# Where the split weights and the split input lie in the on-chip memory of a two-block transformer kernel

## The reference

```python
# block 1
h = rmsnorm(x, norm_mix);  p = h @ w_in                    # 2048 x 4352
x = x + concat([pool_mixer(p), hyena_mixer(p), gated_mixer(p)]) @ w_out
h = rmsnorm(x, norm_ffn);  up = dwconv3(h @ ffn_w_up)      # 2048 x 11264
x = x + (silu(gate) * val) @ ffn_w_down                    # 5632 x 2048
x = rmsnorm(x, norm_final)
# block 2
x = x + rmsnorm(fox_attention(rmsnorm(x, g0), fox_w_in, fox_w_out), g1)
x = x + rmsnorm(square(relu(rmsnorm(x, g2) @ mlp_w1)) @ mlp_w2, g3)   # 2048 x 8192, 8192 x 2048
```

## Time and profile before

| | us |
|---|---|
| three timed runs: median (lowest, highest) | 2157.93 (2157.85, 2158.72) |
| the profiled execution: its own time | 2158.86 |
| the profiled execution: span of the trace | 2157.0 |
| TensorE busy (matmuls) | 2148.6 |
| TensorE's loads of stationary operands, busy | 1864.5 |
| VectorE busy | 1303.6 |
| ScalarE busy | 1009.5 |
| GpSimd busy | 64.5 |

### The profile page before, as it was taken

The page is one execution under the profiler, slowest core; times in us unless marked ns, Lnnn a source line. Parts: engine busy times, 40 slices in busy tenths (PEclk is TensorE's granted clock), DMA queues, the critical chain, the costliest instruction groups (busy, mean ns, idle before and its releaser), DMA issues.

```text
span 2157.0 us, 27987 instructions
## 1 busy us (share of the span) xinstructions
PE 2148.6 (100%) x11694; PEld 1864.5 (86%) x11694; DVE 1303.6 (60%) x1611; ACT 1009.5 (47%) x1186; POOL 64.5 (3%) x85
## 2 busy tenths in 40 slices
PE   9999999999999999999999999999999999999999
PEld 7888888888888888888898889888888888888887
DVE  6868557776777775444655665466555555444445
ACT  6444446545545554444655444455434334444443
POOL 3030000000000000000001010000000000000000
PEclk9999999999999999999999999999999999999999
DMA  9655656566555655555566555546666665555552
GB/s 338 213 172 176 215 183 204 180 196 195 192 184 186 195 181 198 194 194 195 165 205 205 158 176 184 199 144 215 184 189 195 185 188 194 195 195 195 193 190 104
DMA packets 268925, 412.41 MB, mean 191 GB/s; under 512 B 6981, under 2 KB 247045, under 8 KB 250112
## 3 DMA queue, kind: packets, MB, share of 16 engines
q1 hardware_dynamic: 265648, 398.08, 56.6%
q0 software_dynamic: 2432, 11.75, 1.5%
q10 hardware_dynamic: 720, 0.79, 0.1%
HBM read 408.49 MB, written 2.11 MB: 190 GB/s over the span
## 4 chain that ended last, share of the span: by engine, by line
PE 97%; DMA 1%; DVE 1%; ACT 1%; SPq 0%; issue 0%; ACTq 0%; DVEq 0%
PE bank L1546 35%; PE bank L1559 18%; PE bank L1607 11%; PE bank L1608 11%; PE bank L1612 11%; PE bank L1549 2%; PE bank L1561 2%; PE bank L1550 2%; DMA M<-in_xt 1%; PE bank L1441 1%; PE bank L1398 0%; DMA X<-in_x 0%; DVE M L1304 0%; PE bank L1524 0%; PE bank L1491 0%; PE bank L1477 0%
## 5 line engine op out<-in xcount | busy, mean ns | idle before, releaser
L800 DVE TENSOR_TENSOR wlo<-raw,whi 128x2048 fp32r<-128x2048 f32 (+1 forms) x372 | 852.5, 2293 | 760.5 <-ACT whi L480 760.4
L480 ACT ACTIVATE whi<-raw 128x2048 fp32r<-128x2048 f32 (+1 forms) x371 | 710.3, 1916 | 781.5 <-PE bank L1612 421.3
L1546 PE MATMUL bank<-hh,whi 128*128 128x512 f32 x3360 | 807.2, 392 | 0.6 <-ACT whi L480 0.6
L1546 PEld LDWEIGHTS bank<-hh,whi 128*128 128x128 f32 x3360 | 618.3, 188 | 123.5 <-ACT whi L480 1.0
L1559 PEld LDWEIGHTS bank<-hh,wlo 128*128 128x128 f32 x3360 | 430.7, 191 | 16.3
L1559 PE MATMUL bank<-hh,wlo 128*128 128x256 f32 x3360 | 436.0, 283 | 0.0
L1607 PE MATMUL bank<-whi,hh 128*128 128x512 f32 x1072 | 417.6, 390 | 0.0
L1608 PE MATMUL bank<-whi,hh 128*128 128x512 f32 x1072 | 417.1, 389 | 0.0
L1612 PE MATMUL bank<-wlo,hh 128*128 128x512 f32 x1072 | 264.8, 389 | 0.0
L1607 PEld LDWEIGHTS bank<-whi,hh 128*128 128x128 f32 x1072 | 201.2, 188 | 41.9 <-DVE M L868 0.2
L1612 PEld LDWEIGHTS bank<-wlo,hh 128*128 128x128 f32 x1072 | 201.2, 188 | 41.8
(11 more groups left out here) (247 smaller groups left out, 941.8 us busy)
## 6 DMA issues: line engine op xcount, KB each, us to landing
raw<-in_mlp_w SPq DMA_DIRECT2D x128, 1024.0 KB, 5.5
raw<-in_ffn_w_up SPq DMA_DIRECT2D x88, 1024.0 KB, 5.1
raw<-in_ffn_w_down SPq DMA_DIRECT2D x44, 1024.0 KB, 4.8
raw<-in_fox_w_in SPq DMA_DIRECT2D x32, 1024.0 KB, 5.4
raw<-in_w_in SPq DMA_DIRECT2D x31, 1024.0 KB, 5.5
raw<-in_fox_w_in SPq DMA_DIRECT2D x16, 1032.0 KB, 5.4
raw<-in_w_out SPq DMA_DIRECT2D x16, 1024.0 KB, 4.8
raw<-in_fox_w_out SPq DMA_DIRECT2D x16, 1024.0 KB, 4.8
```

The lines of the kernel that those rows point to most:

```text
L480: e.activation(whi[i % RING][:, 0:n], raw[i % RAW][:, 0:n], ACT.Copy).then_inc(s_hi, 1)
L800: e.tensor_tensor(wlo[i % RING][:, 0:n], raw[i % RAW][:, 0:n], whi[i % RING][:, 0:n].bitcast(F), ALU.subtract).then_inc(s_lo, 1)
L1546: e.matmul(bank[b][:, :], wh[:, k, s], hh[:, kk, :], start=kk == 0, stop=False)
```

## The change

The order of the allocations changes, and where the unused bytes stand. All of it is in the list of tensors at the start of `two_block_program`; no instruction is added, removed or moved on any of the five engines, only the addresses in them change (and, by 7, the line numbers behind the list).

```diff
-        st = sb("st", [P, 80])
-        raw = [sb("raw0", [P, UN])]
-        whi, wlo = [], []
-        for i in range(RING):
-            whi.append(sb(f"whi{i}", [P, UN], R))
-            raw.append(sb(f"raw{i + 1}", [P, UN]))
-            gap(2 * i, 96)
-            wlo.append(sb(f"wlo{i}", [P, UN], R))
-            if i == 0:
-                edge = sb("edge", [P, 64])
-            gap(2 * i + 1, 48 if i == 0 else 112)
-        hh = sb("hh", [P, KD, 2 * T], R)
+        tiles = {}
+        for name, before, shape, dt in (
+                ("rb", 0, [P, T], F),
+                ("raw0", 0, [P, UN], F),
+                ("wlo2", 24, [P, UN], R),
+                ("whi2", 32, [P, UN], R),
+                ("whi0", 0, [P, UN], R),
+                ("raw2", 0, [P, UN], F),
+                ("raw3", 0, [P, UN], F),
+                ("cols", 0, [P, NCOL], F),
+                ("wlo0", 72, [P, UN], R),
+                ("wlo1", 0, [P, UN], R),
+                ("edge", 0, [P, 64], F),
+                ("raw1", 0, [P, UN], F),
+                ("hh", 8, [P, KD, 2 * T], R),
+                ("whi1", 0, [P, UN], R),
+                ("st", 0, [P, 80], F),
+                ("end", 24, [P, 8], F)):
+            if before:
+                sb(f"before_{name}", [P, before])
+            tiles[name] = sb(name, shape, dt)
+        st, edge, rb, cols, hh = (tiles[n] for n in ("st", "edge", "rb", "cols", "hh"))
+        raw = [tiles[f"raw{i}"] for i in range(RAW)]
+        whi, wlo = ([tiles[f"{n}{i}"] for i in range(RING)] for n in ("whi", "wlo"))
         hhi, hlo = hh[:, :, 0:T], hh[:, :, T:2 * T]
         X = sb("X", [P, KD, T])
         ident = sb("ident", [P, P])
         onesr = sb("ones", [P, P], R)
         M = sb("M", [P, 18496])
-        cols = sb("cols", [P, NCOL])
         ones = onesr[:, :].bitcast(F)
-        rb = sb("rb", [P, T])
```

More of the change, by code:

```diff
@@ L138, in sem @@
             return ctx.enter_context(nc.semaphore(name))
-        def gap(i, words):
-            sb(f"gap{i}", [P, words])
-        st = sb("st", [P, 80])
-        raw = [sb("raw0", [P, UN])]
-        whi, wlo = [], []
-        for i in range(RING):
-            whi.append(sb(f"whi{i}", [P, UN], R))
-            raw.append(sb(f"raw{i + 1}", [P, UN]))
-            gap(2 * i, 96)
-            wlo.append(sb(f"wlo{i}", [P, UN], R))
-            if i == 0:
-                edge = sb("edge", [P, 64])
-            gap(2 * i + 1, 48 if i == 0 else 112)
-        hh = sb("hh", [P, KD, 2 * T], R)
+        tiles = {}
[22 more added lines that the diff above has]
+        whi, wlo = ([tiles[f"{n}{i}"] for i in range(RING)] for n in ("whi", "wlo"))
         hhi, hlo = hh[:, :, 0:T], hh[:, :, T:2 * T]
```

## The result

The changed kernel takes 2179.28 us (median of three, 2179.2 to 2179.72) against 2157.93: ratio 1.0098, interval 1.0084 to 1.0112. It is slower by 21.4 us, where I had forecast 8.5 us less. That lies above my range (2132 to 2172).

What follows compares the result with a forecast made beforehand. TensorE's matmul pace was taken to bound the kernel. The moved matmuls gave -8.5 us and everything else 0, taking the profiled 2158.9 us to 2150.4, forecast as a median of 2149.5 us; range 2132 to 2172.

Steps and rivals of the forecast that it cites:

- about 8460 matmuls x -1.0 ns: All float32r matmuls with one operand moved off a multiple of 512 bytes: 1.0 ns less each, -8.5 us.
- The upper bound: Sum over the moved matmuls at worst: 8460 x +1.7 ns = +14 us, the range's end at 2172.
- the transposes' 109.4 ns: Time per 128-column transpose, taken as the pace at which loads of the stationary operand can be repeated.
- The 10 ns of cover in line 1559: 256-column matmuls on wlo: a longer stationary load would first have 10 ns spare, 120 against 109.4.
- N/2.4 + 2.5 ns: The Trainium skill's rule for warm matmuls following each other; said to disagree for float32r, agree for plain ones.
- Out of step: Rival, chance 0.29: offsets keep matmul streams in flow "w" and the rows from falling into step, 12 us slower, 2170.
- its first term: Flow "w", stationary operand 32 or 480 bytes off: 1551 matmuls x 4.7 ns = 7.3 us slower.
- the rows' term: Moving operands off the multiple, priced like the slow 258-column row: 2840 x 1.7 ns = 4.8 us slower.
- No address effect on the mean: Rival, chance 0.26: in the float32r matmuls stalls only change their moment, time stays at 2157.9.
- The stall goes: Rival, chance 0.04: an offset removes 11 ns from each of 8460 moved matmuls, 93 us, to 2065.
- the excess: Time per float32r matmul beyond one column per clock: 13.8 ns at 512 columns, 13.3 ns at 256.

Runs made afterwards that it cites:

- The cut matmuls: Kernel before with whi1 at 96 and whi2 at 64 bytes, each 512-column matmul on whi in flow "w" cut into two of 256: 2194.95 us.
- the best of three: Kernel before with wlo written and read 224 bytes further into its buffer in flows "w" and "h": 2149.60 us, ratio 0.9960.

## Why the prediction was wrong

**What bounds the kernel: right.** TensorE's pace is the time, no wait took its place, ScalarE, VectorE and transfers held nothing up, and the raw buffers and small tensors cost nothing (2158.54).

**That addresses change the pace: right, and for the reason half seen.** I said that the distance between the two starts might be what matters; the kernel with everything at 32 shows it.

**The step that failed** is the term "about 8460 matmuls x -1.0 ns". I read the 1.0 ns from matmuls of 258 columns and put it on all moved matmuls alike. For the 3360 of line 1559, with 256 columns, it was the right sign and too small: 1.88 us for 16 against 1.91, about 2 ns each, 6 us gained. For the 512-column matmuls it was wrong in sign: 2256 in flow "w" lost (3.73 - 3.65) / 16 = 5 ns each, 11 us; the rows lost 18.5 us. The cut matmuls show that this goes with the number of columns and not with reading `whi`; nor is it the moving of both halves of `hh`, which the rows don't do. For 24 matmuls of the rows I had 5.42 us; they took 5.54 to 5.60.

**The upper bound failed with it.** It was the worst row of a 258-column unit, +1.7 ns, again from another number of columns. The 512-column matmuls gave +5 ns in flow "w" and +6 to +8 in the rows (1.88 us for the 8 on `wlo1` against 1.82). With +14 us as the highest sum the range ended at 2172.

**What runs ahead was put at nothing.** I priced only the matmuls whose own operands moved. But the 16 on the unmoved `whi1` of the rows took 3.66 us instead of 3.63, and when `wlo` alone was moved the untouched `whi` matmuls of flow "w" took up to 3.68 instead of 3.65; in that kernel this came to 8 us. A distance is also felt by the matmuls behind it. It can help too: in flow "w" of the changed kernel the units with `whi1` took 3.64.

**A reading that does not stand.** I took the transposes' 109.4 ns for the pace of the stationary load. On the page of before, a transpose of 128 columns lasts 274 ns, as long as a plain matmul of 128 columns (275), and one of 384 columns lasts 486 ns. That is 0.83 ns per column, two clocks:

```profile
L1398 PE MATMUL bank<-ident,X 128*128 128x128 f32 x96 | 12.1, 274 | 0.5 <-DVE X L1310 0.5
L1477 PE MATMUL bank<-M 128*128 128x384 f32 x16 | 5.5, 486 | 0.0
```

By that the columns of a transpose take 107 ns by themselves, and no row shows a load that sets a pace. The 10 ns of cover in line 1559 had no ground; no term of the sum used it. I also wrote that the plain matmuls agree with N/2.4 + 2.5 ns. They do in the 2.5 ns alone: with one clock per column 384 columns would take 162.5 ns, and they take 322.5.

**The rivals.** "Out of step" named the mechanism nearest to what happened, with its first term near the mark (7.3 us against 11) and the rows' term far too small (4.8 against 18.5), for the same reason as above: 2170 instead of 2179. I gave it 0.29. The starts in the trace after bear its picture out: in flow "w" the matmuls on `whi0` go on alternating between 232 and 235 ns to the end of the unit, while those on `whi1` are at 227 from the third on. Its sign could have been read: the aligned 512-column matmuls run evenly, and the first five of each unit, not yet in step, take 232 ns. That was the only 512-column row of before out of its even pace, and it pointed upward. I gave the 258-column row the sum and this one a rival.

"No address effect on the mean" fell. The Trainium skill ("TensorE: Matmul & The Clock Gate", section "Step-by-step: what each phase is for") has the stationary load take no bandwidth from the stream, through a read port of its own. These runs disagree to this extent: the pace depends on where one read starts in relation to the other, for 512 columns by up to 3% in flow "w" and 4% in the rows (5.68 us against 5.44), and for 256 by up to 5%. "The stall goes" fell as well; the largest part of the excess that any distance took away is 6 ns of 13 (1.82 us for 16), for 256 columns only.

## What to carry to other kernels

If TensorE is busy all the time, read the distance from one matmul's start to the next, per buffer, and compare it with the columns at the granted clock; a layout shows up as units of a different length for each ring buffer. For float32r keep stationary and moving operands at the same offset within 256 bytes where the moving operand has 512 columns; no other distance was safe in both flows. With 256 columns some other distance is better, and it can be set per phase inside the buffer; here the best of three gave 0.4%. Measure it in place, because the matmuls ahead have their say. A price read at one number of columns is no price at another: bound it from a row of the same shape, or leave the bound wide.

## What the runs showed of the hardware

- The pace of float32r matmuls depends on the distance between the starts of their two operands, not on either start (0 and 32 for all: 2158.3 and 2158.14 us), and in flow "w" a distance of 256 bytes did as 0 (3.65 and 1.91 us).
- In flow "w", distances of 16, 32, 48, 64, 96, 128, 192, 224, 288, 320, 384 and 480 bytes slow 512 columns (3.71 to 3.75 us for 16 instead of 3.65), and 496 does not (3.64). For 256 columns the distances tried, other than 160 and 256, take 1.82 to 1.90 us for 16 instead of 1.91; 160 took up to 1.92.
- In the rows, where the weights move, 496 is the slowest distance (5.68 us for 24 matmuls of 512 columns against 5.44 at 0).
- Which pace sets in can depend on what ran ahead: 256 columns at distance 64 took 113.8 ns behind 512-column ones at 64 (1.82 us for 16) and 118 behind those at 0 (1.89). At 224 they took 1.87 us behind either.
- Half the stationary columns left the pace of 512 moving columns nearly as it was (3.67 against 3.65 us for 16).
